# Block products with seven multiplications in place of eight for 18 of 22 up-projection chunks, and product splits moved to the down stage

## The chip, the cores and the metric

The kernel runs on one core of one Trainium2 chip. The metric is the time of one execution on the device in microseconds, as the median of the runs; the profile is of one more execution. The engines are named as in the profile: PE (TensorE, matmuls), DVE (VectorE), ACT (ScalarE), POOL (GpSimd) and SP (SyncE, which here issues the loads).

## The reference

Two layers of a streaming encoder act on 544 rows (512 of a prompt and 32 of a running stream). The first half of a layer (three gated branches and a projection) is untouched by the change. The second half is a gated channel mixer with D_MODEL = 1024 and D_FF = 2816:

```python
f_gate, f_val = jnp.split(x @ w_up, 2, axis=-1)
ffn_ext = jnp.concatenate([ffn_hist.astype(f_gate.dtype), f_gate], axis=1)
f = jax.nn.gelu(causal_dwconv(ffn_ext, ffn_conv_w, ffn_conv_b), approximate=False) * f_val
x = layer_norm(DN_ALPHA * x + f @ w_down, ln2_g, ln2_b)
```

The convolution has width 3 along the rows. All of it is float32.

## The kernel before, in words

**Number format.** Every matmul operand is split into a high part (a copy of type float32r, named wh, xh, fhh) and a low part (the rest: the float32 value minus the high one, named wl, xl, fll). A product is three matmuls into the same PSUM bank: high by high, low x by high weights, high x by low weights (`three`, lines 1683 to 1691). Features lie on the partitions and the 544 rows of x along the free dimension, in two halves of HALF = 272 (dcol(0) and dcol(1)).

**Weight ring.** All weights come as chunks of up to 128 x 2048 float32. SP loads a chunk into `raw[s]` (L339) when the slot is free, ACT copies it to `wh[s]` (`hi`, L505), DVE subtracts into `wl[s]`, which lies on top of `raw[s]` (`lo`, L998), and PE uses it. There are three slots in this stage. POOL makes the low part of one chunk per layer in four pieces of 512 (L482) and is otherwise used for masks, and for four subtractions in the tail (L489).

**Up stage.** An up chunk holds 256 output channels (two tiles of 128, m = 0 and 1) by 1024 inputs (eight tiles). Chunks alternate: a gate chunk, then the value chunk of the same channels; there are 11 pairs per layer. `chunk` on PE makes four units from one: two output tiles by two halves of rows, each 8 x 3 = 24 matmuls into a bank of its own, so 96 per chunk. The first three chunks (gate 0, value 0, gate 1) are taken half by half, because the second half of x is normalised while PE works on the first; the fourth and the 18 that follow are whole.

**Behind a pair.** ACT copies the four gate banks into `gex` (`gate_rows`, L866 to L869), applies the first tap into `cbuf` (`conv_open`, L877), DVE adds the two other taps (`conv_close`, L1551 and L1557), ACT applies the gelu (L881), DVE multiplies with the value banks into `tmp` (`f_products`, L1574 to L1579), ACT copies the high part into `fhh` (`f_rows`, L886) and DVE the low part into `fll` (`f_lows`, L1585). All of it stands in a fixed order written out per engine; ACT and DVE work strictly in that order.

**Down stage.** `down` is called four times per layer (two halves of rows by two halves of the output channels). Each time it takes six chunks (KGROUPS = 3, 4, 3, 4, 4, 4 tiles of inputs) into four banks, 264 matmuls. The first call waits for the products of all pairs but the last before it begins, and for the last pair before its sixth chunk. Then the second layer norm follows beside the calls.

## Time and profile before

| | |
|---|---|
| median of 3 runs | 1798.47 us (1798.11 to 1800.48) |
| span of the profiled execution, first to last instruction | 1796.6 us |
| between that span and the median | 1.9 us |
| PE busy | 1783.3 us, 99% |
| DVE busy | 1141.6 us, 64% |
| ACT busy | 773.2 us, 43% |
| POOL busy | 101.0 us, 6% |
| DMA | 186.00 MB, mean 104 GB/s |

A record of an instruction runs from its start to its end as the profiler saw it. Consecutive records of one engine overlap a little, and matmuls overlap much, so PE's pace is read from counts in a stretch and not from the length of a record. An instruction that is held up by something other than a semaphore has started in the record, so its record is longer; an instruction that waits for a semaphore has not.

### The profile page before, as it was taken

What the parts mean: (1) busy time and instruction counts of PE and PEld (TensorE: products, weight loads), DVE (VectorE), ACT (ScalarE), POOL (GpSimd) and SP (SyncE); (2) the same over time, 40 slices, a digit from 0 to 9 for tenths busy, and PEclk for the clock granted to TensorE, in tenths of its full rate; (3) what the DMA queues carried; (4) which work ended last, traced back from release to release, by engine and by line L of the source; (5) the groups of instructions that cost most, each with busy time, mean ns of one, the idle gap of its engine ahead of it and who ended that gap; (6) DMA issues with size and microseconds to landing.
All of it is one profiled execution on the core that took longest, in us unless ns stands there. A gap on an engine that the chain in (4) does not pass through costs nothing.

```text
span 1796.6 us, 32671 instructions
## 1 busy us (share of the span) xinstructions
PE 1783.3 (99%) x14234; PEld 1749.4 (97%) x14234; DVE 1141.6 (64%) x1745; ACT 773.2 (43%) x1260; POOL 101.0 (6%) x159
## 2 busy tenths in 40 slices
PE   9999999999999999999999999999999999999997
PEld 9998999999999999999999989999999999999997
DVE  5798787755764444446668886786558644445565
ACT  4256533353453344434542564324535534444343
POOL 0025100000100000000000350000001000000000
PEclk9999999999999999999999999999999999999999
DMA  4522122223222222255525221222222222222544
GB/s 172 170 96 72 54 78 83 94 72 116 96 71 82 84 95 95 68 177 181 170 92 169 74 93 38 83 94 78 99 106 71 92 74 94 94 85 94 182 165 137
DMA packets 36511, 186.00 MB, mean 104 GB/s; under 512 B 7376, under 2 KB 11728, under 8 KB 18192
## 3 DMA queue, kind: packets, MB, share of 16 engines
q1 hardware_dynamic: 34672, 176.28, 29.0%
q10 hardware_dynamic: 1696, 7.64, 1.2%
q8 instruction: 112, 1.84, 0.4%
q14 instruction: 31, 0.25, 0.1%
HBM read 176.75 MB, written 7.15 MB: 102 GB/s over the span
## 4 chain that ended last, share of the span: by engine, by line
PE 96%; DVE 3%; issue 1%; DMA 0%; ACT 0%; ACTq 0%; DVEq 0%
PE acc L1685 29%; PE acc L1690 29%; PE acc L1691 29%; PE score L1761 1%; PE small L1812 1%; PE turned L1792 1%; DVE acc L1202 1%; PE score L1690 1%; PE score L1691 1%; PE score L1685 1%; PE turned L1854 1%; PE score L1978 0%; DMA raw<-win 0%; PE small L1827 0%; PE score L1771 0%
## 5 line engine op out<-in xcount | busy, mean ns | idle before, releaser
L1685 PE MATMUL acc<-xh,wh 128*128 128x272 f32 x2944 | 857.0, 291 | 1.5 <-DVE xl L952 1.3
L1690 PE MATMUL acc<-xl,wh 128*128 128x272 f32 x2944 | 847.5, 288 | 0.0
L1691 PE MATMUL acc<-xh,wl 128*128 128x272 f32 x2944 | 847.1, 288 | 0.0
L1685 PEld LDWEIGHTS acc<-xh,wh 128*128 128x128 f32 x2944 | 554.4, 188 | 9.1 <-issue 5.7
L1690 PEld LDWEIGHTS acc<-xl,wh 128*128 128x128 f32 x2944 | 554.2, 188 | 0.1
L1691 PEld LDWEIGHTS acc<-xh,wl 128*128 128x128 f32 x2944 | 553.0, 188 | 0.0
L998 DVE TENSOR_TENSOR wl<-raw,wh 128x2048 fp32r<-128x2048 f32 (+2 forms) x154 | 318.4, 2068 | 215.6 <-ACT wh L505 215.0
L505 ACT ACTIVATE wh<-raw 128x2048 fp32r<-128x2048 f32 (+2 forms) x174 | 305.2, 1754 | 180.5 <-DMA raw<-wdn 132.7
L1685 PE MATMUL acc<-fhh,wh 128*128 128x272 f32 x704 | 204.1, 290 | 0.0
L1691 PE MATMUL acc<-fhh,wl 128*128 128x272 f32 x704 | 202.7, 288 | 0.0
L1690 PE MATMUL acc<-fll,wh 128*128 128x272 f32 x704 | 202.3, 287 | 0.0
L1202 DVE SCALAR_TENSOR_TENSOR acc<-glu,par,acc 128x574 f32<-128x574 f32 x240 | 181.1, 813 | 0.1
L1551 DVE SCALAR_TENSOR_TENSOR cbuf<-gex,par,cbuf 128x546 f32<-128x546 f32 x44 | 34.5, 784 | 197.9 <-ACT cbuf L877 197.9
L1685 PEld LDWEIGHTS acc<-fhh,wh 128*128 128x128 f32 x704 | 132.6, 188 | 0.2
L1690 PEld LDWEIGHTS acc<-fll,wh 128*128 128x128 f32 x704 | 132.5, 188 | 0.2
L1691 PEld LDWEIGHTS acc<-fhh,wl 128*128 128x128 f32 x704 | 132.3, 188 | 0.0
L783 ACT ACTIVATE tmp<-acc,par 128x272 f32<-128x272 f32 x96 | 46.6, 488 | 196.1 <-PE acc L1691 195.7
L1685 PE MATMUL acc<-mh,wh 128*128 128x272 f32 x256 | 74.9, 292 | 0.0
L1691 PE MATMUL acc<-mh,wl 128*128 128x272 f32 x256 | 73.7, 288 | 0.0
L1690 PE MATMUL acc<-ml,wh 128*128 128x272 f32 x256 | 73.7, 288 | 0.0
L886 ACT ACTIVATE fhh<-tmp 128x272 fp32r<-128x272 f32 x88 | 35.2, 431 | 82.0 <-DVE tmp L1579 42.3
L1147 DVE TENSOR_TENSOR_SCAN keep<-keep,zero 128x128 f32<-128x128 f32 (+4 forms) x68 | 58.6, 861 | 15.3 <-POOL beta L471 12.5
(268 smaller groups left out, 2279.2 us busy)
## 6 DMA issues: line engine op xcount, KB each, us to landing
raw<-win SPq DMA_DIRECT2D x50, 1024.0 KB, 4.9
raw<-wup SPq DMA_DIRECT2D x44, 1024.0 KB, 4.9
raw<-wdn SPq DMA_DIRECT2D x32, 1024.0 KB, 4.9
raw<-wbr SPq DMA_DIRECT2D x24, 512.0 KB, 3.6
raw<-wdn SPq DMA_DIRECT2D x16, 768.0 KB, 4.2
raw<-wout SPq DMA_DIRECT2D x8, 1024.0 KB, 4.9
v_out<-vfm ACTq DMA_DIRECT2D x2, 1088.0 KB, 8.7
k_out<-k ACTq DMA_DIRECT2D x2, 1088.0 KB, 4.9
```

Of the source, the lines that this page charges most:

```text
L505: A(wh[s][:, 0:n], raw[s][:, 0:n], ACT.Copy).then_inc(hi_full[s], c.up(hi_full[s]))
L783: A(tmp[:, b, :], ps[b][:, 0:HALF], ACT.Sigmoid, bias=col(par, PAR["b_gate"] + 8 * BRANCHES[n] + 2 * i + b % 2)).then_inc(acc_free[b], c.u ...
L886: A(row(fhh[b // 2], 2 * i + b % 2, 0, HALF), tmp[:, b, :], ACT.Copy).then_inc(f_hi, c.up(f_hi))
L998: v.tensor_tensor(wl[s][:, 0:n], raw[s][:, 0:n], wh[s][:, 0:n].bitcast(F32), ALU.subtract).then_inc(lo_full[s], c.up(lo_full[s]))
L1147: v.tensor_tensor_scan(keep[b][:, T - w:T][:, ::-1], keep[b][:, T - w:T][:, ::-1], zero[:, 0:1].broadcast_to([P, w]), 1.0, ALU.mult, ALU.a ...
L1202: v.scalar_tensor_tensor(out=acc[:, m, :], in0=glu_at(m, j), scalar=w, in1=acc[:, m, :], op0=ALU.mult, op1=ALU.add).then_inc(vec, c.up(vec))
L1551: v.scalar_tensor_tensor(out=cbuf[:, m, :], in0=gex[:, m, 1:GEX - 1], scalar=col(par, PAR["fw"] + FT + t), in1=cbuf[:, m, :], op0=ALU.mult ...
L1685: first = mm(out, a, xs[0], start=start, stop=False)
L1690: mm(out, a, xs[1], start=False, stop=False)
L1691: return mm(out, b, xs[0], start=False, stop=stop)
L1761: last = mm(bs[b][:, 0:w], yc[x][rows, ht, i * P:w], ks[y][rows, ht, 0:w], start=x + y == 0, stop=y == 1)
L1792: last = pe.transpose(bt[:, kb * P:(kb + 1) * P], beta[n % 2][part][:, kb * P:(kb + 1) * P], ident[:, :])
```

## The change

**The products.** 18 chunks per layer (gate 2 to 10 and value 2 to 10) are computed as a 2 x 2 block product. Write the chunk as blocks a11, a12 (output tile 0, first and second four input tiles), a21, a22 (output tile 1), and x as b11, b12 (first four tiles, two halves of rows) and b21, b22. In place of eight block products of four tiles each there are seven (`products`), after sums

```text
s1 = a21 + a22   a3 = a11 - a21   s2 = s1 - a11   s4 = a12 - s2
t1 = b12 - b11   t3 = b22 - b12   t2 = b22 - t1   t4 = b21 - t2
product 1 a11*b11   2 a12*b21   3 s2*t2   4 a3*t3   5 s1*t1   6 s4*b22   7 a22*t4
```

Products 1 and 2 are accumulated in different banks and added by DVE for c11; product 3 is accumulated onto 1, 5 onto 3 and 6 onto 5, with copies m1, u1 and u3 of the bank by ACT in between; 4 has a bank of its own onto which 7 is accumulated (c22 = product 4's bank + u3 is taken by DVE between them, c21 = the bank after 7 + u1). c12 is the bank after product 6. `ORDER` puts products 1 and 2 of the next chunk between 5, 6 and 7 of this one.

**The sums.** The x sums (t1 to t4, each 4 x 272 wide) are made by POOL once per layer when all of x is there, and split by ACT and DVE. The weight sums (s1, a3, s2, s4, each 4 x 128 = 512 wide) are made by POOL per chunk; a3 replaces a21 in `raw[s]`, s1, s2, s4 go to `sraw` and are split by ACT (`shi`) and DVE (`slo`), two at once and then one. The high part of a chunk is two copies of 1024 (second blocks, then first blocks after a3).

**The order.** On ACT per chunk: u3 of the chunk before, high part of the second blocks of the next, m1, c12 of the chunk before, high part of the first blocks, the sums' high parts, u1. On DVE: c22 of the chunk before, c11, first low part of the next, c21 of the chunk before, the other lows. Conv, gelu and gating stand between them.

**The down stage.** The gated products are kept as float32 (`f32`) and split in groups of four tiles (FGROUPS, last one two): for the first half of rows at the end of the up stage, for the second half during the first calls of `down`. `down` waits for the groups it is about to use.

```diff
+QUADS = 18
+ORDER = [(0, 1), (0, 2)]
+for _q in range(QUADS):
+    ORDER += [(_q, 3), (_q, 4), (_q, 5)]
+    ORDER += [(_q + 1, 1)] if _q + 1 < QUADS else []
+    ORDER += [(_q, 6)]
+    ORDER += [(_q + 1, 2)] if _q + 1 < QUADS else []
+    ORDER += [(_q, 7)]
...
+                pool.wait_ge(x_ready[0], 16 + 16 * r)
+                pool.wait_ge(x_ready[1], 16 + 16 * r)
+                x_at = [[xT[:, 4 * k_:4 * k_ + 4, dcol(h)] for h in range(2)] for k_ in range(2)]
+                for n, (j, a, b) in enumerate(((T1, x_at[0][1], x_at[0][0]), (T3, x_at[1][1], x_at[0][1]),
+                                               (T2, x_at[1][1], traw[T1][:, :, :]), (T4N, x_at[1][0], traw[T2][:, :, :]))):
...
+                    g.tensor_tensor(traw[j][:, :, :], a, b, ALU.subtract).then_inc(t_made, 1)
...
+                    pool.wait_ge(raw_full[s], 16 * (SLOT[:j + 1].count(s) - (1 if s < 2 else 0)))
+                    if q > 1:
+                        pool.wait_ge(prod_full, full_at(r, q - 2, 5))
+                    g.tensor_tensor(s1, a21, a22, ALU.add).then_inc(s_made, 1)
+                    pool.wait_ge(s_made, made + 1)
+                    g.tensor_tensor(a21, a11, a21, ALU.subtract).then_inc(s_made, 1)
+                    g.tensor_tensor(s2, s1, a11, ALU.subtract).then_inc(s_made, 1)
+                    pool.wait_ge(s_made, made + 3)
+                    if q > 1:
+                        pool.wait_ge(prod_full, full_at(r, q - 2, 6))
+                    g.tensor_tensor(s4, a12, s2, ALU.subtract).then_inc(s_made, 1)
```

On PE, `products` waits at the head of a product:

```diff
+                    if p == 2:
+                        pe.wait_ge(lo_full[blocks[q]], c.take(lo_full[blocks[q]]))
...
+                    if p == 3:
+                        pe.wait_ge(snapped, act_at(r, "m1", q))
+                        pe.wait_ge(s_ready, sums + 1)
...
+                    if p == 5:
+                        pe.wait_ge(snapped, act_at(r, "u1", q))
+                    if p == 6:
+                        pe.wait_ge(snapped, act_at(r, "u3", q))
+                        pe.wait_ge(s_ready, sums + 2)
+                    if p == 7:
+                        pe.wait_ge(combined, dve_at(r, "c22", q))
```

On DVE, at the first pairs and at the end of the stage:

```diff
                 history(0)
                 conv_close(0)
                 f_products(0, FIRST_VALUE)
                 lo()
-                f_lows(0)
-                for i in range(10):
...
+                turned_x_lo()
+                history(1)
+                first_low(0)
+                skip(range(4))
+                conv_close(1, range(2), False)
+                other_lows(0)
+                f_products(1)
...
+                for g_ in range(1, 3):
+                    f_lows(0, g_)
+                lo()
+                for g_ in range(3, 6):
+                    f_lows(0, g_)
```

On PE, in `down`:

```diff
-                        if h == 0 and j == len(KGROUPS) - 1:
-                            pe.wait_ge(f_ready, c.seen(f_ready))
+                        groups = [g_ for g_, (a, b) in enumerate(FGROUPS) if a < at + kn]
+                        pe.wait_ge(f_ready, 12 * r + 6 * h + groups[-1] + 1)
```

The order of the instructions shows three places. On POOL, behind the low part of the chunk that it had before (wl), there were the masks of the next layer:

```order
L482 TENSOR_TENSOR wl_60<-raw_57,wh_54 128x512 [waits hi_full2]
L482 TENSOR_TENSOR wl_60<-raw_57,wh_54 128x512 x3
L462 AFFINE_SELECT wsgu<-wsgu 128x512 [waits late_full]
L471 AFFINE_SELECT keep_111<-keep_111 128x128 [waits sig_full0]
L471 AFFINE_SELECT beta_113<-beta_113 128x128
```

and now the x sums (traw) and the weight sums (sraw, and raw in place for a3) stand between them:

```order
L546 TENSOR_TENSOR wl_60<-raw_57,wh_54 128x512 x3
L556 TENSOR_TENSOR traw_101<-xT 128x1088 [waits x_ready1,x_ready0]
L556 TENSOR_TENSOR traw_100<-xT 128x1088
L556 TENSOR_TENSOR traw_99<-xT,traw_101 128x1088 [waits t_made]
L556 TENSOR_TENSOR traw_102<-xT,traw_99 128x1088 [waits t_made]
L569 TENSOR_TENSOR sraw_105<-raw_55 128x512 [waits raw_full0]
L571 TENSOR_TENSOR raw_55<-raw_55 128x4x128 [waits s_made]
L572 TENSOR_TENSOR sraw_105<-sraw_105,raw_55 128x512
L576 TENSOR_TENSOR sraw_105<-raw_55,sraw_105 128x512 [waits s_made]
```

The four of a chunk come 18 times per layer, from the third chunk on with waits for prod_full too. On DVE a pair in the middle of the stage was

```order
L1557 SCALAR_TENSOR_TENSOR cbuf<-gex,par,cbuf 128x546 [waits vec]
L998 TENSOR_TENSOR wl_58<-raw_55,wh_52 128x2048 [waits hi_full0]
L1574 TENSOR_TENSOR tmp<-acc,cbuf 128x272 [waits fgelu_full,acc_full0]
L1574 TENSOR_TENSOR tmp<-acc,cbuf 128x272 [waits fgelu_full,acc_full1]
L1577 TENSOR_TENSOR tmp<-acc,cbuf 128x240 [waits acc_full2]
L1579 TENSOR_TENSOR tmp<-acc,cbuf 128x32
L1577 TENSOR_TENSOR tmp<-acc,cbuf 128x240 [waits acc_full3]
L1579 TENSOR_TENSOR tmp<-acc,cbuf 128x32
L1585 TENSOR_TENSOR fll_87<-tmp,fhh_85 128x272 [waits f_hi] x2
L1585 TENSOR_TENSOR fll_88<-tmp,fhh_86 128x272 [waits f_hi] x2
L998 TENSOR_TENSOR wl_59<-raw_56,wh_53 128x2048 [waits hi_full1]
```

and of one chunk now, from the gating products on (f is the float32 product, small and turned are banks, m and u the copies by ACT):

```order
L1845 TENSOR_TENSOR f_89<-f_89,cbuf 128x544 [waits fgelu_full,snapped,combined]
L1846 TENSOR_TENSOR f_90<-f_90,cbuf 128x2x240
L1847 TENSOR_TENSOR f_90<-f_90,cbuf 128x2x32
L1813 TENSOR_TENSOR wl_58<-raw_55,wh_52 128x1024 [waits s_made]
L1818 TENSOR_TENSOR slo_108<-sraw_106,shi_104 128x1024 [waits s_hi]
L1818 TENSOR_TENSOR slo_108<-sraw_106,shi_104 128x512 [waits s_hi]
L1826 TENSOR_TENSOR gex<-small,u_0_111 128x240 [waits snapped,prod_full]
L1827 TENSOR_TENSOR gex<-small,u_0_111 128x32
L1837 TENSOR_TENSOR f_89<-acc,m_1_112 128x272 [waits snapped,prod_full]
L1806 TENSOR_TENSOR wl_59<-raw_56,wh_53 128x1024 [waits s_made,hi_full1]
L1837 TENSOR_TENSOR gex<-small,u_0_110 128x272 [waits snapped,prod_full]
```

One low part of 2048 has become three of 1024 and one of 512 with waits between them, and the narrow products and splits have gone. At the end of the stage, DVE goes from the last chunk to the down chunks (wl of 2048 is the second down chunk) in this order:

```order
L1837 TENSOR_TENSOR f_89<-turned,u_1_113 128x272 [waits snapped,prod_full]
L1845 TENSOR_TENSOR f_89<-f_89,cbuf 128x544 [waits fgelu_full,snapped,combined]
L1846 TENSOR_TENSOR f_90<-f_90,cbuf 128x2x240
L1847 TENSOR_TENSOR f_90<-f_90,cbuf 128x2x32
L1788 TENSOR_TENSOR fll_87<-f_89,fhh_85 128x1088 [waits f_hi] x2
L1199 TENSOR_TENSOR wl_59<-raw_56,wh_53 128x2048 [waits hi_full1]
L1788 TENSOR_TENSOR fll_87<-f_89,fhh_85 128x1088 [waits f_hi] x2
```

Before, both low parts of the first two down chunks stood ahead of the last pair's products. PE has 13203 rows in its order, where it had 13635.

## Rows read from the trace of the kernel before

**Rows 1.** Page of the profile: busy time per engine, and the chain that ended last.

```profile
PE 1783.3 (99%) x14234; PEld 1749.4 (97%) x14234; DVE 1141.6 (64%) x1745; ACT 773.2 (43%) x1260; POOL 101.0 (6%) x159
...
PE 96%; DVE 3%; issue 1%; DMA 0%; ACT 0%; ACTq 0%; DVEq 0%
```

**Rows 2.** Stretches of the up stage: busy us of PE, PEld, DVE, ACT, POOL; clock, DMA.

```profile
545.10:761.60 216.50, 216.50 (x1729) 216.50 (x1729) 100.90 (x199) 88.43 (x144) 0.00 (x0) 1.00 0.25 87
1433.60:1650.00 216.40, 216.40 (x1729) 216.40 (x1728) 100.74 (x200) 88.67 (x145) 0.00 (x0) 1.00 0.25 87
```

**Rows 3.** DVE groups by form (busy us, mean ns), and four rows in order of time.

```profile
L998 DVE TENSOR_TENSOR wl<-raw,wh 128x1024 fp32r<-128x1024 f32 x24 | 29.3, 1221 | 14.7 <-ACT wh L505 14.7
L1551 DVE SCALAR_TENSOR_TENSOR cbuf<-gex,par,cbuf 128x546 f32<-128x546 f32 x44 | 34.5, 784 | 197.9 <-ACT cbuf L877 197.9
L1125 DVE TENSOR_TENSOR sq<-xT,st 128x544 f32<-128x544 f32 x32 | 21.9, 725 | 0.4
L1048 DVE TENSOR_TENSOR xT<-xT,small 128x1088 f32<-128x1088 f32 x8 | 10.2, 1280 | 0.0
...
617.75 1.49 DVE L1585 TENSOR_TENSOR fll<-tmp,fhh 128x272 fp32r<-128x272 f32 x4
```

**Rows 4.** ACT groups by form (busy us, mean ns).

```profile
L505 ACT ACTIVATE wh<-raw 128x2048 fp32r<-128x2048 f32 x134 | 256.1, 1911 | 121.3 <-DMA raw<-wdn 94.2 <-DMA raw<-win 20.3 <-DMA raw<-wout 4.6
L505 ACT ACTIVATE wh<-raw 128x1024 fp32r<-128x1024 f32 x24 | 25.3, 1054 | 20.7 <-DMA raw<-wbr 20.7
L639 ACT ACTIVATE wh<-raw 128x512 fp32r<-128x512 f32 x4 | 2.5, 627 | 2.4 <-DMA raw<-win 2.4
L866 ACT ACTIVATE gex<-acc 128x272 f32<-128x272 f32 x40 | 15.6, 396 | 51.3 <-PE acc L1691 51.3
```

**Rows 5.** POOL's pieces at 484 us and DVE beside them (start, us), and one DVE line.

```profile
484.19 1.66 POOL L482 TENSOR_TENSOR wl<-raw,wh 128x512 fp32r<-128x512 f32 x1 [296.61 <-ACT wh L505]
485.81 1.49 POOL L482 TENSOR_TENSOR wl<-raw,wh 128x512 fp32r<-128x512 f32 x1
488.50 1.28 POOL L482 TENSOR_TENSOR wl<-raw,wh 128x512 fp32r<-128x512 f32 x1
...
483.98 0.73 DVE L1037 TENSOR_TENSOR cbuf<-xT 128x544 f32<-128x544 f32 x1
484.74 1.41 DVE L1039 TENSOR_TENSOR st<-cbuf 128x272 f32<-128x272 f32 x1
...
L1039 DVE TENSOR_TENSOR st<-cbuf x8: 441/443/1418, 458.6 to 1751.8; 128x272 f32<-128x272 f32 x8
```

**Rows 6.** Loads of the up weights: count, size, median us from issue to landing.

```profile
raw<-wup SPq DMA_DIRECT2D x44, 1024.0 KB, 4.9
```

**Rows 7.** The tail: POOL's subtractions and DVE beside them.

```profile
1785.82 1.29 POOL L489 TENSOR_TENSOR xT<-xT,cbuf 128x272 f32<-128x272 f32 x1 [407.79 <-ACT cbuf L938]
1788.99 0.75 POOL L489 TENSOR_TENSOR xT<-xT,cbuf 128x272 f32<-128x272 f32 x1
...
1786.42 0.43 DVE L1111 TENSOR_TENSOR st<-turned,st 128x272 f32<-128x272 f32 x1
1786.77 0.93 DVE L1116 TENSOR_TENSOR xT<-xT,cbuf 128x544 f32<-128x544 f32 x1
```

**Rows 8.** Start of the up stage: DVE, and ACT's read of a gate bank.

```profile
514.58 0.44 DVE L1131 TENSOR_TENSOR xl<-xT,xh 128x272 fp32r<-128x272 f32 x1 [0.57 <-ACT xh L543]
...
522.42 0.79 DVE L1551 SCALAR_TENSOR_TENSOR cbuf<-gex,par,cbuf 128x546 f32<-128x546 f32 x1 [7.24 <-ACT cbuf L877]
...
528.38 2.29 DVE L998 TENSOR_TENSOR wl<-raw,wh 128x2048 fp32r<-128x2048 f32 x1 [0.47 <-ACT wh L505]
...
533.07 0.37 ACT L868 ACTIVATE gex<-score 128x240 f32<-128x240 f32 x1 [2.54 <-PE score L1691]
```

**Rows 9.** End of the up stage: DVE's low part of the second down chunk.

```profile
758.25 2.29 DVE L998 TENSOR_TENSOR wl<-raw,wh 128x2048 fp32r<-128x2048 f32 x1 [0.86 <-ACT wh L505]
```

More of the change, by code:

```diff
@@ L1542, in _, with conv_close @@
                 low_tiles(1, range(KT))
[L1545 to L1548 removed]
+                def conv_close(i, tiles=range(2), counted=True):
+                    if counted:
+                        skip(range(4))
+                    for m in tiles:
                         t = 2 * i + m
@@ new lines, in left @@
+                def left(q, m):
+                    i = 2 + q // 2
+                    bank, add = (PA[q % 2], snap[q % 2]["m1"]) if m == 0 else (PC[q % 2], snap[q % 2]["u1"])
+                    dve.wait_ge(prod_full, full_at(l, q, 7 if m else 2))
+                    dve.wait_ge(snapped, act_at(l, "u1" if m else "m1", q))
+                    out = gex[:, m, 2:2 + HALF] if q % 2 == 0 else f32[0][:, 2 * i + m, :]
+                    v.tensor_tensor(out, bank[:, 0:HALF], add[:, :], ALU.add).then_inc(combined, 1)
@@ L2040, in _, with products @@
                 chunk()
-                for r in range(9):
-                    chunk()
-                    chunk()
+                blocks = {}
+                def products(n):
+                    q, p = ORDER[n]
+                    bank = {1: PB, 6: PB, 7: PC, 2: PA, 3: PB, 4: PC, 5: PB}[p][q % 2]
+                    sums = 2 * (r * QUADS + q)
+                    if p == 1:
+                        blocks[q] = arrived()
+                        if q > 1:
+                            pe.wait_ge(snapped, act_at(r, "c12", q - 2))
+                    if p == 2:
+                        pe.wait_ge(lo_full[blocks[q]], c.take(lo_full[blocks[q]]))
+                        if q > 1:
+                            pe.wait_ge(combined, dve_at(r, "c11", q - 2))
+                        else:
+                            pe.wait_ge(acc_free[q], c.seen(acc_free[q]))
+                    if p == 3:
+                        pe.wait_ge(snapped, act_at(r, "m1", q))
+                        pe.wait_ge(s_ready, sums + 1)
+                        if q == 0:
+                            pe.wait_ge(t_ready, 4 * (r + 1))
+                    if p == 4 and q > 1:
+                        pe.wait_ge(combined, dve_at(r, "c21", q - 2))
+                    if p == 5:
[5 more added lines that the diff above has]
+                        pe.wait_ge(combined, dve_at(r, "c22", q))
+                    s, half = blocks[q], q % 2
+                    for t in range(4):
+                        if p in (1, 2, 4, 7):
+                            at = {1: t * 256, 2: (4 + t) * 256, 4: t * 256 + P, 7: (4 + t) * 256 + P}[p]
+                            w = [x[s][:, at:at + P] for x in (wh, wl)]
+                        else:
+                            w = [x[half][:, {5: 0, 3: 1, 6: 2}[p], t * P:(t + 1) * P] for x in (shi, slo)]
+                        if p in (1, 2, 6):
+                            tile, h = {1: (t, 0), 2: (4 + t, 0), 6: (4 + t, 1)}[p]
+                            mv_ = [x[:, tile, dcol(h)] for x in xs]
+                        else:
+                            mv_ = [x[{3: T2, 4: T3, 5: T1, 7: T4N}[p]][:, t, :] for x in (th, tl)]
+                        last = three_of(bank[:, 0:HALF], w, mv_, p in (1, 2, 4) and t == 0, t == 3, p not in (1, 2, 4))
+                    last.then_inc(prod_full, 1)
+                    if p == 7:
+                        read.append(s)
@@ L2046, in down @@
+                for n in range(len(ORDER)):
+                    products(n)
+                pe.wait_ge(combined, dve_at(r, "c11", QUADS - 1))
                 def down(h, middle=None):
```

314 lines of the change are left out of this document (265 added, 49 removed).

## The prediction, made before the change was timed

> **What bounds the kernel now.** I read the busy times of the page first. TensorE (PE) is busy in 99% of the span and the chain that ended last runs 96% through it [rows 1]; every other engine has slack on average. Then the stretches of the up stage [rows 2]: in the first layer PE fills all of 545.1 to 761.6 us, and the second layer repeats it from 1433.6 to 1650.0. These 216.5 us are 18 chunks of 96 matmuls, so a matmul costs 216.5 / 1728 = **0.1253 us**, and a chunk 12.03 us. The granted clock is 1.00 there, the upper level of 2.4 GHz, and PE did not pause. POOL does nothing in that stretch, DVE is busy 100.9 and ACT 88.4 of 216.5 us. So a matmul taken out is worth its 0.1253 us as long as the other engines keep up with the new, shorter chunk.
>
> **What is taken out.** A chunk is a 2 by 2 block product (two halves of the input rows by two output tiles, with two column halves). Eight block products of 12 matmuls become seven: 84 matmuls, 10.52 us. Per layer 18 x 12 x 0.1253 = **27.06 us**, for two layers 54.1. The order of the instructions agrees: PE has 432 rows fewer.
>
> **What is added, engine by engine, for one chunk of 10.52 us.** "Takes" is a record less the 0.08 us by which neighbours overlap, as where four 272-wide DVE rows of 0.43 us take 1.49 [rows 3].
> - ACT: 88.4 / 18 = 4.9 us a chunk before. The high half of 2048 (1.91 us) becomes two of 1.05, and the sums of 1024 and 512 add 1.05 and 0.63 [rows 4]; the bank reads (0.40) are about as many as before. That is 6.8 us of 10.52, off the path.
> - DVE: two lows of 1024 (1.22), lows of the sums of 1024 and 512 (1.22, 0.69), three additions that read PSUM (0.44, as the 272-wide row of rows 5), and per pair four conv steps (0.79), gating products of 544, 480 and 64 (0.73 for 544, estimated 0.66 and 0.2) and small copies [rows 3]. Taken together 7.6 us.
> - POOL: four additions or subtractions of 512. The nearest row is its own low half of 512, 1.28 us alone, one every 1.24 [rows 5]. That is 5.0 us.
> - DMA: one load of 1 MB per chunk as before, 4.9 us to landing [rows 6]. The slot is freed at product 7 and the sums are first wanted three products (4.5 us) later, so POOL starts some 0.4 us late; it is inside the POOL chain below.
>
> No engine is full by itself. **But DVE and POOL get in each other's way.** At 484.19 us POOL begins its first piece while DVE runs a 544-wide subtraction until 484.71. The piece takes 1.66 instead of 1.28 us and ends at 485.85. DVE's next addition (272 wide, both inputs in SBUF) starts at 484.74 and takes 1.41 instead of 0.44 us: it ends at 486.15, 0.30 us after the piece. POOL's second piece then ends at 487.30, 1.15 after that [rows 5]. The tail repeats it (DVE 0.93 instead of 0.73 us beside POOL's 272-wide subtractions, 1.29 instead of 0.75 [rows 3, 7]). So an instruction of POOL and a DVE instruction with two SBUF inputs exclude each other; a hold is 1.15 us for POOL's 512, and for DVE its record less about 0.13. DVE instructions that read a PSUM bank are not held (0.43 at 1786.42, beside POOL [rows 7]).
>
> Per chunk the holds are: POOL 4 x 1.15 = 4.6; DVE lows 3 x 1.09 + 0.56 = 3.8, conv 2 x 0.66 = 1.3, gating 0.6 (half a pair), 5.7 together. **10.3 of 10.52 us**: the pair is full to 98%. The Trainium skill ("SBUF — State Buffer", section "SBUF: two separate sides") says that of such a pair whichever starts first has the shared ports for the whole instruction. Read as whole records, that rule would make 11.8 us of the 10.3; the trace agrees that one blocks the other, and differs in the length, since DVE ends 0.30 us behind the piece where its record alone is 0.44 [rows 5].
>
> What does the 98% cost PE? By the bounds: nothing, if the waits fall in DVE's own pauses; and if DVE stood still through all of POOL's holds, its chunk would be 7.6 + 4.6 = 12.2 us, 1.7 over PE's. About 1.5 us of DVE's work (the PSUM additions and the copies) can run beside POOL, which leaves 10.7, 0.2 over. I take **0.35 us** a chunk: those 0.2 and 0.15 for moments in which both wait for a product. PE would show it before product 7 (it needs the bottom-right addition of DVE) and before product 5 (it needs ACT's copy u1, which is queued behind the high halves of POOL's sums). The last two chunks of a layer have no sums beside them, so 16 x 0.35 = 5.6 us per layer.
>
> **The start of the stage.** POOL now makes four combinations of x, 1088 wide, as soon as the last low tile of x is there (515.0 [rows 8]). From its 512 and 272 wide rows (1.28 and 0.75 alone, 2.2 ns an element) one takes an estimated 2.4 to 2.5 us, so they last until 524.6, and the eight sums of two chunks follow without pause. DVE's four conv steps of the first pair start at 522.4 [rows 8] and each now waits for one POOL instruction, 2.2 + 3 x 1.15 = 5.7 us. Behind them stand ACT's gelus, ACT's high half and DVE's low half of the second value chunk, which was ready at 530.67 for a unit that PE began when the one before ended, at 533.07 [rows 8]: 2.4 us of slack. So PE waits 3.3 us (bounds: 0 if POOL is slower to start than the conv, 5.7 if it also collides with the low half). Behind that, ACT and DVE still have the splits of the combinations to do, but 12 us of units cover them.
>
> **The end of the stage.** Before, the low half of the second down chunk ran at 758.25 and was done 1.1 us before the stage ended [rows 9]. Now it stands behind the last product. From the last product's end DVE does: latency 0.2, bottom-left addition 0.4, gating products 1.4, two splits of four tiles (1088 wide, 1.2 each, from the 1.28 of the same width [rows 3]), the low half 2.2. That is 6.6 us; PE has 36 matmuls of the first down chunk, 4.5 us. **2.1 us** of wait (0 to 3.5). The other product splits are cheaper than before (six wide ones for 22 narrow) and covered by the down stage's passes of 264 matmuls, 33 us each.
>
> **The sum.** Per layer 27.06 - 5.6 - 3.3 - 2.1 = 16.06 us, twice 32.1. The profiled span is 1796.6 us, and 1.9 us lie between it and the median 1798.47, which I carry along: 1764.5 span, **1766.4 us**.
>
> **Rivals.**
> 1. *The exclusion hides.* For it: DVE was idle for more than half of the up stage [rows 2], and the additions have two chunks of lead. Against: 98%. Then only the 2.1 us at the end stay: 1798.5 - 2 x (27.06 - 2.1) = 1748.6 us.
> 2. *An instruction holds for its whole record*, its fixed part included: POOL 4 x 1.28 and DVE 6.7 (three of 1.22, 0.69, two of 0.79, gating 0.8) make a chunk of 11.8 us, 1.3 over PE's. Per layer 27.06 - 16 x 1.3 - 5.4 = 0.9, so 1796.7 us, no difference. The row of 484.74 is against it. It is what the page of the Trainium skill named above would make of it.
> 3. *The chain through POOL sets the pace*, and the kernel is slower. Place: product 5 of chunk q - 2 ends, POOL does four operations, ACT the last high half and u1, and only then product 5 of chunk q - 1 may start. Besides POOL this chain has 0.2 + 0.6 + 0.4 + 0.4 for the late load + 1.6 for the product, 3.2 us; it keeps PE's pace if POOL needs under 7.3 us. Alone it needs 5.0; if each operation also waits for one DVE low (1.09) it needs 4 x (1.15 + 1.09) = 9.0, a chunk of 12.2 us. Per layer 27.06 - 16 x 1.7 - 5.4 = -5.5, so 1809.5 us. It turns to a loss at a chunk of 11.9, POOL at 8.7 us. For it: POOL here reads blocks with gaps, which no row shows, and it collides at every step. Against: of DVE's nine holds in a chunk at least half fall outside these 7 us.
>
> That the change does not do what it says is ruled out by the order's 432 rows. Met waits at the head of each product are counted at nothing: the stage before has four of them a chunk, and PE is busy in 216.50 of 216.50 us [rows 2].
>
> **Chances.** Forecast (0.1 to 0.9 us lost per chunk) 0.55, rival 1 0.25, rival 2 0.07, rival 3 0.13. A measurement of this kernel can tell about 0.2%, 3.6 us. Faster by more: 0.55 + 0.25 + 0.03 of rival 2 (it stands at the bound) = 0.83; within: 0.04 of rival 2 and 0.02 from the mild end of rival 3; slower 0.11. Range: down to 1746, 2.6 us under rival 1 for an end that hides too; up to 0.95 us lost per chunk, 2 x 16 x 0.6 = 19 us over the forecast, 1786. Rivals 2 and 3 stay outside.
>
> **What would show it.** Right: PE has 84 matmuls in 10.7 to 11.0 us in the middle of the stage; POOL's 512-wide rows read 1.3 to 2.3 us, not 1.28, and DVE's 1024-wide lows up to 2.4 instead of 1.22; PE waits before a product on DVE (small or turned) or ACT (u1), together 5 to 6 us per layer, and once 2 to 4 us near the second value chunk and about 2 us on the low half of the second down chunk. Wrong: POOL at 1.28 throughout (rival 1); a chunk over 11.5 us with ACT's u1 as the releaser (rival 3); POOL over 1.6 us where no DVE instruction runs beside it, which my prices do not have.

## The result and the profile after

The changed kernel takes **1813.36 us** (median of four runs, 1811.58 to 1816.19) where the kernel before took 1798.36 beside it: a ratio of 1.0084, 95% interval 1.007 to 1.0098. It is slower; 1766.4 was predicted, with 0.11 on slower. The profiled span is 1810.6 us, 14.0 over the span before, where 54.1 us of matmuls had been taken out. So 68 us went elsewhere, 34 per layer; the prediction had allowed 11.

The page after (busy time, and the chain that ended last), against [rows 1]:

```profile
PE 1754.7 (97%) x13802; PEld 1709.7 (94%) x13802; DVE 1348.9 (75%) x1869; ACT 850.5 (47%) x1366; POOL 345.0 (19%) x311
...
PE 74%; DVE 12%; issue 4%; DMA 4%; ACT 3%; POOL 3%; ACTq 0%; DVEq 0%; POOLq 0%
```

PE did lose work, but it is busy for 97% and no longer 99% of the span, and the chain leaves it for a quarter of the way, mostly to DVE. PE's waits after (engine line waited for: us in total, times, longest us); before, the whole list came to 2.7 us:

```profile
PE score L1978 <- ACT u L1016: 21.4, 18, 2.5
PE acc L1978 <- ACT gex L962: 6.4, 2, 3.2
PE acc L1978 <- DVE wl L1199: 6.2, 5, 2.1
PE acc L1978 <- DVE f L1777: 6.2, 2, 3.7
```

A wait costs PE somewhat more than the list says, since the first matmul starts late too: 1.14 us in the list is a start 1.43 us behind the start before it, 1.30 more than the usual 0.125.

**In the middle of the stage** PE stops once per pair of chunks, before product 6 of the odd chunk:

```profile
622.14 0.29 PE L1984 MATMUL score<-xh,wl 128*128 128x272 f32 x1
623.57 0.39 PE L1978 MATMUL score<-xh,shi 128*128 128x272 f32 x1 [1.14 <-ACT u L1016]
```

The next such stop begins at 645.16. A pair thus takes 23.02 us, a chunk 11.51: the change wanted 10.52 and the kernel before took 12.03. **0.99 us a chunk** is lost where 0.35 was priced. Of the 2.0 us of a pair the stop and the slow start behind it are 1.4; the rest are stops of 0.1 to 0.3 us before product 7 and before product 5. What stood ahead of the wait is seen on three engines (start, us, in order of time). DVE:

```profile
615.83 2.35 DVE L1806 TENSOR_TENSOR wl<-raw,wh 128x1024 fp32r<-128x1024 f32 x1 [0.48 <-POOL sraw L572]
...
618.45 1.21 DVE L1813 TENSOR_TENSOR wl<-raw,wh 128x1024 fp32r<-128x1024 f32 x1
619.58 1.81 DVE L1818 TENSOR_TENSOR slo<-sraw,shi 128x1024 fp32r<-128x1024 f32 x2
621.32 0.23 DVE L1767 COPY gex<-fhist 128x2 f32<-128x2 f32 x2
622.54 0.86 DVE L1753 SCALAR_TENSOR_TENSOR cbuf<-gex,par,cbuf 128x546 f32<-128x546 f32 x1 [1.00 <-ACT cbuf L1034]
```

ACT:

```profile
621.66 1.58 ACT L1034 ACTIVATE cbuf<-gex,par 128x546 f32<-128x546 f32 x2 [3.32 <-DVE gex L1767]
623.15 0.37 ACT L1016 ACTIVATE u<-score 128x272 f32<-128x272 f32 x1
```

POOL:

```profile
615.80 1.28 POOL L576 TENSOR_TENSOR sraw<-raw,sraw 128x512 f32<-128x512 f32 x1
621.54 1.28 POOL L569 TENSOR_TENSOR sraw<-raw 128x512 f32<-128x512 f32 x1 [4.45 <-DMA raw<-wup]
```

POOL's 615.80 holds DVE's low part, 2.35 us instead of 1.21. From there DVE's queue runs on without pause, so the tiny history copies (L1767), which stand last in it, come at 621.32. ACT has been idle for 3.32 us with its next instruction, the first tap of the conv (L1034), waiting for them. Behind the two taps on ACT stands u3, and on u3 waits product 6.

The groups show how far the exclusion reaches. DVE after, by form (busy us, mean ns); the last two are copies of two columns, the same work, 0.16 us each in the kernel before. They stand one behind the other, so that the first bears the whole hold:

```profile
L1806 DVE TENSOR_TENSOR wl<-raw,wh 128x1024 fp32r<-128x1024 f32 x36 | 60.4, 1677 | 7.3 <-POOL sraw L572 7.3
...
L1756 DVE COPY fst<-gex 128x2 f32<-128x2 f32 x44 | 33.5, 762 | 0.0
L1757 DVE COPY fst<-gex 128x2 f32<-128x2 f32 x44 | 6.9, 156 | 0.0
```

POOL's sums take means of 1.41 to 1.69 us, 6.2 for the four of a chunk; two of the four groups:

```profile
L569 POOL TENSOR_TENSOR sraw<-raw 128x512 f32<-128x512 f32 x36 | 60.6, 1685 | 204.3 <-DMA raw<-wup 158.1 <-PE score L1984 46.2
L572 POOL TENSOR_TENSOR sraw<-sraw,raw 128x512 f32<-128x512 f32 x36 | 50.8, 1412 | 0.0
```

**At the start and the end** PE waits three times per layer. In the first layer (start, us):

```profile
536.87 0.57 PE L1978 MATMUL acc<-xh,wh 128*128 128x272 f32 x1 [3.21 <-ACT gex L962]
555.82 0.36 PE L1978 MATMUL acc<-xh,wh 128*128 128x272 f32 x1 [2.51 <-DVE f L1777]
770.69 0.39 PE L1978 MATMUL acc<-fhh,wh 128*128 128x272 f32 x1 [2.12 <-DVE wl L1199]
```

Measured from start to start these are 3.50, 2.80 and 2.41 us (3.46, 3.94 and 2.42 in the second layer). ACT and DVE around the first two:

```profile
531.40 4.09 ACT L982 ACTIVATE th<-traw 128x1088 fp32r<-128x1088 f32 x4
535.40 1.04 ACT L993 ACTIVATE wh<-raw 128x1024 fp32r<-128x1024 f32 x1
536.35 0.66 ACT L962 ACTIVATE gex<-acc 128x272 f32<-128x272 f32 x2
```

```profile
533.74 9.21 DVE L1795 TENSOR_TENSOR tl<-traw,th 128x1088 fp32r<-128x1088 f32 x4
546.97 1.25 DVE L1756 COPY fst<-gex 128x2 f32<-128x2 f32 x1
```

Behind some of these waits PE runs at its lower clock level. One window of the profile after (busy us of PE, PEld, DVE, ACT, POOL; granted clock, DMA):

```profile
496.00:545.00 49.00, 45.61 (x336) 44.69 (x335) 39.25 (x53) 27.25 (x46) 21.91 (x10) 0.93 0.19 65
```

### The profile page after: what moved, and what is told of

Read it like the earlier page. It is cut to its first block, busy times and chain, and to the rows that moved or that the text cites. A ratio compares the mean times of both kernels' runs of the same rounds, so it can differ in the third digit from the quotient of the medians.

```text
span 1810.6 us, 32645 instructions
## 1 busy us (share of the span) xinstructions
PE 1754.7 (97%) x13802; PEld 1709.7 (94%) x13802; DVE 1348.9 (75%) x1869; ACT 850.5 (47%) x1366; POOL 345.0 (19%) x311
## 4 chain that ended last, share of the span: by engine, by line
PE 74%; DVE 12%; issue 4%; DMA 4%; ACT 3%; POOL 3%; ACTq 0%; DVEq 0%; POOLq 0%
PE acc L1978 21%; PE acc L1984 20%; PE acc L1983 20%; DMA raw<-wup 3%; PE score L1978 2%; DVE slo L1818 2%; PE score L1984 2%; PE score L1983 2%; POOL sraw L569 1%; PE score L2054 1%; DVE wl L1199 1%; PE small L2105 1%; PE turned L2085 1%; DVE wl L1813 1%; DVE cbuf L1753 1%
## 5 line engine op out<-in xcount | busy, mean ns | idle before, releaser
L1978 PE MATMUL acc<-xh,wh 128*128 128x272 f32 x1936 | 570.6, 295 | 14.0 <-ACT gex L962 6.4
L1984 PE MATMUL acc<-xh,wl 128*128 128x272 f32 x1936 | 560.9, 290 | 0.0
L1983 PE MATMUL acc<-xl,wh 128*128 128x272 f32 x1936 | 559.9, 289 | 0.0
L1978 PEld LDWEIGHTS acc<-xh,wh 128*128 128x128 f32 x1936 | 367.5, 190 | 22.4 <-issue 18.3
L1199 DVE TENSOR_TENSOR wl<-raw,wh 128x2048 fp32r<-128x2048 f32 (+2 forms) x118 | 236.0, 2000 | 179.4 <-ACT wh L601 178.8
L1983 PEld LDWEIGHTS acc<-xl,wh 128*128 128x128 f32 x1936 | 367.7, 190 | 0.1
L1984 PEld LDWEIGHTS acc<-xh,wl 128*128 128x128 f32 x1936 | 366.7, 189 | 0.0
L1978 PE MATMUL score<-th,shi 128*128 128x272 f32 x288 | 85.4, 297 | 2.2 <-ACT u L1016 2.2
L1984 PE MATMUL score<-th,slo 128*128 128x272 f32 x288 | 83.5, 290 | 0.0
L1983 PE MATMUL score<-tl,shi 128*128 128x272 f32 x288 | 83.0, 288 | 0.0
```

The lines of the kernel that those rows point to most:

```text
L1199: v.tensor_tensor(wl[s][:, 0:n], raw[s][:, 0:n], wh[s][:, 0:n].bitcast(F32), ALU.subtract).then_inc(lo_full[s], c.up(lo_full[s]))
L1978: first = mm(out, a, xs[0], start=start, stop=False, skip_group_check=onto)
L1983: mm(out, a, xs[1], start=False, stop=False, skip_group_check=onto)
L1984: return mm(out, b, xs[0], start=False, stop=stop, skip_group_check=onto)
```

## The experiments

Two things were in question. One is the exclusion between POOL and DVE: seen rightly, but under-priced. The other is the new order of the work (history copies last on DVE, taps ahead of u3 on ACT), which might cost the time by itself, with or without POOL. Each expectation says what its own A and B are. The four runs with memsets are single executions; the four runs of the change lie up to 4.6 us apart, so differences of 1 us between single runs say nothing.

**The exclusion taken away, the order kept.** POOL takes as long as its sums would take alone, in steps with the same waits, but as memsets, which read nothing. From the third chunk on the weight sums are not computed.

```diff
+                    if q >= 2:
+                        for n in range(4):
...
+                            pool.wait_ge(s_made, made + n)
+                            g.memset(scratch[:, 0:680], 0.0).then_inc(padded, c.up(padded))
+                            pool.wait_ge(padded, c.seen(padded))
+                            g.memset((s1, scratch[:, 0:512], s2, s4)[n], 0.0).then_inc(s_made, 1)
+                        return
```

> From the third chunk of a layer on POOL's four sums are replaced by pairs of memsets of the same length (about 1.3 us a pair, with the same semaphores), which read nothing; the weight sums are not computed. Theory B: with nothing of POOL to exclude, DVE is on time, the chunk falls from 11.5 to 10.5 us and the time by 32 x 1.0 = 31 us to about 1782. Theory A: DVE runs some 1 us per chunk earlier, so the history copies and u3 come earlier too, but they still stand behind the lows that wait for POOL's last sum; at most half of the loss goes, 1798 us or more.

1778.71 us, 34.7 less than the change. A pair of memsets takes what a sum took alone, start to start 1.31 us (5.2 us for the four, where the held sums needed 6.2):

```profile
626.23 0.67 POOL L576 MEMSET scratch<- 128x680 f32 x1 [5.69 <-DMA raw<-wup]
626.96 0.53 POOL L578 MEMSET sraw<- 128x512 f32 x1
627.54 0.67 POOL L576 MEMSET scratch<- 128x680 f32 x1
```

DVE's low part after a3 is back at the price of [rows 3], and PE's waits on ACT's copies are 3.0 us where they were 21.4 (line numbers are 11 higher here: the two copies are L1756 and L1757 of the change):

```profile
L1817 DVE TENSOR_TENSOR wl<-raw,wh 128x1024 fp32r<-128x1024 f32 x36 | 43.8, 1217 | 3.8 <-POOL sraw L578 3.8
L1767 DVE COPY fst<-gex 128x2 f32<-128x2 f32 x44 | 19.8, 451 | 0.0
L1768 DVE COPY fst<-gex 128x2 f32<-128x2 f32 x44 | 18.5, 419 | 0.0
...
PE score L1989 <- ACT u L1027: 3.0, 4, 0.8
```

The exclusion from the third chunk on is worth 17.3 us per layer (half of 34.7), against 5.6 priced. The Trainium skill ("SBUF — State Buffer", section "Who interferes with whom") says that a DVE instruction with two SBUF inputs contends with a GpSimd instruction that reads SBUF and not with one that only writes, and that a copy can run in a mode in which it contends with GpSimd whatever that does. The run agrees on both: 1677 ns fell to 1217, but the two copies, 762 and 156 ns in the change, are at 451 and 419. Together they still take 870 ns, where they took 918, and 0.32 us before. So the memsets free all of DVE but its copies.

**The same, and the history copies early.**

```diff
                     if q < QUADS:
                         left(q, 0)
+                    if q % 2 == 0 and q < QUADS:
+                        dve.wait_ge(conv3_full, c.seen(conv3_full))
+                        history(2 + q // 2)
                     first_low(q + 1)
...
                     if q % 2:
-                        history(2 + q // 2)
```

> Both edits: history copies early, and POOL's sums replaced by memsets of the same length (weight sums not computed). Both theories: every wait inside the stage goes, a chunk of 10.5 us, and only the waits at the start (about 3.4 and 3.3 us), at the end (2.4) and the half-rate stretches behind them stay: about 1782 us. If it is clearly above, there is a third cause in the chain of POOL, ACT and PE itself.

1779.71 us with the memsets, no gain. Once POOL's reads hold nobody, the order costs nothing, so it is not a cause by itself. Whether it decides how much of the holds reaches PE is the question of the next run.

**The history copies early, POOL as in the change.**

> Only DVE's two history copies (2 columns each) into gex move: from behind the low parts of the next chunk to right after the addition for c11 of the even chunk. Theory A (the steady loss is an ordering: the copies are last in DVE's queue, ACT's taps wait for them, u3 stands behind the taps, product 6 waits for u3): the 1.43 us gap before product 6 of every odd chunk goes, 8 pairs x 2 layers x about 1.4 us = 22 us, so about 1791 us. Theory B (POOL and DVE exclude each other and DVE is simply late): the taps start earlier but DVE stays late, another wait (product 5 or 7) takes its place, and at most 8 us are won, 1805 us or more.

1801.59 us, ratio to the kernel before 1.0013 (1.0004 to 1.0022): 12 us won, between the two expectations. The wait before product 6 is gone, and two others have come:

```profile
PE score L1980 <- ACT u L1016: 14.7, 15, 1.1
PE small L1980 <- DVE gex L1827: 2.9, 12, 0.9
```

The first is now before product 5, on u1. At one such place (ACT, then POOL, then DVE):

```profile
626.10 0.66 ACT L1039 ACTIVATE cbuf<-cbuf 128x546 f32<-128x546 f32 x1 [1.92 <-DVE cbuf L1759]
626.67 1.04 ACT L1005 ACTIVATE shi<-sraw 128x1024 fp32r<-128x1024 f32 x1
628.13 0.38 ACT L1016 ACTIVATE u<-score 128x272 f32<-128x272 f32 x1
```

```profile
623.49 1.66 POOL L576 TENSOR_TENSOR sraw<-raw,sraw 128x512 f32<-128x512 f32 x1
```

```profile
620.44 1.81 DVE L1759 SCALAR_TENSOR_TENSOR cbuf<-gex,par,cbuf 128x546 f32<-128x546 f32 x1
622.52 1.47 DVE L1753 SCALAR_TENSOR_TENSOR cbuf<-gex,par,cbuf 128x546 f32<-128x546 f32 x1
623.92 1.26 DVE L1756 COPY fst<-gex 128x2 f32<-128x2 f32 x1
```

POOL's last sum was there at 625.15, and ACT could not take it, since the gelu ahead of it in its queue waited for DVE's conv, in which POOL had held two steps and two copies. Of the 16 odd chunks from chunk 3 on (counted from 0), ACT takes the last sum 2.1 to 2.5 us after POOL has made it in 13; in the even ones it takes it at once and then waits for PE. So it is not POOL's chain that is long; DVE is full. The same 23 us of the stage in this run, in the memset run and in the change (busy us of PE, PEld, DVE, ACT, POOL; clock, DMA):

```profile
604.20:627.20 23.00, 21.69 (x171) 21.25 (x169) 22.41 (x29) 13.05 (x22) 12.52 (x8) 1.00 0.28 95
```

```profile
604.20:627.20 23.00, 23.00 (x185) 23.00 (x184) 17.29 (x31) 14.19 (x24) 10.46 (x18) 1.00 0.28 94
```

```profile
604.20:627.20 23.00, 21.86 (x170) 21.26 (x169) 20.26 (x29) 12.74 (x22) 12.16 (x9) 1.00 0.27 93
```

DVE's records fill 22.41 of 23.00 us in the first, 5.1 more than in the memset run. In the change it is 20.26, with pauses in which ACT's taps run. In the memset run PE is never idle.

The 12 us did not come from the pairs in the middle of the stage. The first matmul of product 6 of chunks 5 and 15 in this run (in the change they start at 623.57 and 739.05):

```profile
619.75 0.29 PE L1980 MATMUL score<-xh,shi 128*128 128x272 f32 x1
...
734.38 0.29 PE L1980 MATMUL score<-xh,shi 128*128 128x272 f32 x1
```

That is 11.46 us a chunk, and 11.55 in the change; six chunks of the second layer give 11.42 and 11.48. With the copies early more of DVE's instructions run into POOL's: over one pair the held records exceed their price alone by 7.2 us together, where it was 5.0 in the change. So what were pauses is now filled with holds. The bulk of the 12 us lies in the first pairs of each layer (3.4 and 2.6 us between product 6 of chunk 0 and that of chunk 5), at the end of the second layer's stage (2.9, where a wait of 2.82 us with a stretch at half rate is gone).

**The start.** All 18 chunks with memsets, the x sums real (the weight sums are not computed):

```diff
-                    if q >= 2:
+                    if q >= 0:
```

> POOL's weight sums of all 18 chunks are memset pairs of equal length (they read nothing, the weight sums are not computed); the x sums stay real. With the earlier run in which the first two chunks kept real sums (1778.7) and the one in which the x sums were memsets too (1761.4) it splits the loss at the start. Theory A (the second wait comes from DVE's low parts of the x sums, 9.2 us for four, each held by POOL's eight sums of the first two chunks): they take 5.1 us now, the second wait of 3.9 goes, the first (ACT's splits wait for POOL's late x sums, which collide with the conv) stays at 2 to 3.5: 1767 to 1771. Rival B (it comes from the late x sums alone): both waits stay, 1776 to 1779.

1768.66 us, 10.1 less than with two chunks left real. DVE's four low parts of the x sums and PE's first wait:

```profile
533.43 4.89 DVE L1806 TENSOR_TENSOR tl<-traw,th 128x1088 fp32r<-128x1088 f32 x4
...
536.56 0.36 PE L1989 MATMUL acc<-xh,wh 128*128 128x272 f32 x1 [3.22 <-ACT gex L973]
```

They take 4.89 instead of 9.21 us. The second wait is gone, the first stands. So the second is made by the weight sums of the first two chunks, which the prediction had all but over by then: it let them follow the x sums "without pause", but POOL waited for the load of that chunk until 532.67 and so met the low parts.

Then the x sums as memsets of equal length too (neither kind of sum is computed):

```diff
-                    g.tensor_tensor(traw[j][:, :, :], a, b, ALU.subtract).then_inc(t_made, 1)
+                    for w in (760, 760):
+                        g.memset(scratch[:, 0:w], 0.0).then_inc(padded, c.up(padded))
+                        pool.wait_ge(padded, c.seen(padded))
+                    g.memset(traw[j][:, :, :], 0.0).then_inc(t_made, 1)
```

> As the memset run, with all of POOL's work of this stage replaced by memsets of equal length: the x sums and the sums of the first two chunks too (no block sums are computed). If the two waits at the start of the stage (3.5 us on ACT's read of a gate bank, 3.9 us on DVE's products of the second value chunk) come from the exclusion as well, the first falls to about 1 us and the second goes, with the stretches at half rate behind them: 2 x (2.5 + 3.9 + 1 to 2) less than the 1778.7 us of the memset run, 1762 to 1766 us. If they come from the order in ACT's and DVE's queues, it stays at 1775 us or more.

1761.37 us, another 7.3 less; the first wait falls from 3.50 to 1.47 us. The exclusion, but for the copies, is thus worth 52.0 us, 26 per layer. What is left, 17.1 us of span over 1796.6 - 54.1, is there without it, 1.47 us of the first wait too.

ACT's gate reads ahead of the splits of the x sums, in the change itself:

```diff
+                for b in range(2):
+                    gate_rows(b, SECOND_GATE[b])
                 turned_x_hi()
                 second_blocks(0)
-                for b in range(4):
+                for b in range(2, 4):
                     gate_rows(b, SECOND_GATE[b])
```

> ACT reads the first two gate banks of the second pair ahead of the splits of the x sums and of the high half of the next chunk; nothing else is changed. Theory A (the two waits at the start are one delay that is handed on: the DVE low parts of the x sums, 9.2 us for four, stand in both): the first wait falls from 3.5 to about 0.5 us and the second grows by about as much (2.8 and 3.9 to 6 to 7), so the time stays within 3 us of the change, 1810 to 1816. Rival B (the second wait has causes of its own, ACT's order was the whole of the first): the second stays 2.8 to 3.9, 3 us are won per layer and the half-rate stretch behind the first goes too: 1803 to 1807.

1813.07 us, no difference. The first wait fell to 0.46 us, the second grew to 8.45 in both layers, from 2.80 and 3.94 (in the list, two waits on DVE's f of 16.3 us together). The waits are one delay that is handed on; with no stop before it, PE only reaches the second place earlier.

Gates early, DVE's products of the second value chunk ahead of its other low parts, history early and the end of the next paragraph, all at once:

> The history copies early, and three more moves: ACT reads the first two banks of the second gate chunk before it splits the x sums, DVE takes the products of the second value chunk before the low parts of the sums, and the second down chunk's high and low halves go before the last chunk's work. Theory A plus the reading of the trace (the waits of 3.5, 2.8 to 3.9 and 2.4 us at the edges come from these three places, and each is followed by a stretch at half rate that costs 1.4 to 2.5 us more): 1791 less 2 x (3.4 + 2.4 + 1.6 for the half rate) or more, 1775 us; 1768 if the second wait goes as well. Rival for the edges: DVE is behind by the excluded time and only the releaser changes, 1785 or more.

1797.89 us, 0.9994 (0.9984 to 1.0003): 3.7 less than with history early alone, which is about what the end is worth. At the start the wait became one of 7.69 us per layer, on another low part. Moving work about does not help while DVE is held.

**The end.** Both parts of the second down chunk split ahead of the last chunk's additions, the low one on DVE as shown, the high one on ACT likewise:

```diff
+                    if q == QUADS:
+                        lo()
                     first_low(q + 1)
...
                 for g_ in range(1, 3):
                     f_lows(0, g_)
-                lo()
```

> Only the end of the stage is changed: both halves of the second down chunk are split ahead of the last chunk's additions. Theory A (the term of the end stands by itself): the wait on wl of 2.4 us becomes one of 1.25 on the split of the products, as where this was done with other edits; 1.2 us are won per layer, and the half-rate stretch behind the wait (about 1.3 us lost) goes too: 5 us in all, 1807 to 1810. Rival B (the time lost at half rate is not owed to the length of the wait): 2.4 us in all, 1810.5 to 1812.

1809.26 us, 1.0061 (1.0044 to 1.0077), 4.1 less than the change. The wait is 1.28 us in place of 2.41. This is 2.3 us for two layers; the half-rate stretch behind the wait is gone too, but the change had one in the first layer only (last section), 1.4 us. The sum is 3.7. That it comes so near to 4.1 is in part chance: elsewhere this trace has a half-rate stretch that is longer by 1.2 us and lacks the wait of 2.82.

**Less for POOL to do.** History early, and s2 and s4 made by DVE. POOL keeps s1 and a3:

```diff
-                    g.tensor_tensor(s2, s1, a11, ALU.subtract).then_inc(s_made, 1)
...
-                    g.tensor_tensor(s4, a12, s2, ALU.subtract).then_inc(s_made, 1)
...
+                def own_sums(q):
...
+                        v.tensor_tensor(s2, s1, a11, ALU.subtract).then_inc(s_dve, 1)
+                        dve.wait_ge(s_dve, 2 * (l * QUADS + q) + 1)
+                        v.tensor_tensor(s4, a12, s2, ALU.subtract).then_inc(s_dve, 1)
```

> History copies early, and two of the four weight sums of a chunk (s2 and s4) are made by DVE in place of POOL. Exclusion theory, with the holds read before the change: POOL 2 x 1.15 and DVE 5.7 + 2 x 0.55 are 9.1 us in place of 10.3 for a chunk of 10.52, while DVE has 8.8 us of work of its own in place of 7.6. Most of the steady waits go, 1801.6 less some 20: 1778 to 1786 us. If what counts is DVE's amount of work, the time rises above 1801.6; if it is the length of the chain from product 5 through POOL, it falls too, but the memset run (same length of chain, no waits) speaks against that.

1777.07 us, 0.988 (0.9867 to 0.9894): 24.5 less than history early alone, and faster than before. DVE, the engine that was full, got two more instructions a chunk (0.69 us each), and the kernel became faster, because each takes one of POOL's holds away: over the whole kernel DVE's records come to 1362.5 us, and to 1374.4 with history early alone, though 49.8 us of work were added to them. POOL's chain is shorter here too; that this was not the limit rests on the last sums that waited for ACT above, not on this run.

History early and the x sums made by DVE, which is idle there; ACT's splits of them move ahead of its last gate reads of the first pair (not shown):

```diff
                 history(0)
+                turned_x()
+                turned_x_lo()
                 conv_close(0)
                 f_products(0, FIRST_VALUE)
                 lo()
-                turned_x_lo()
```

> History copies early, and the four x sums are made and split on DVE and ACT in the 7 us in which DVE was idle before the first conv step, in place of POOL beside the conv steps. Only the start of the stage changes: the waits of 3.5 and 3.9 us and the half-rate stretches behind them go or shrink to under 2 us, 1801.6 less 2 x 7 to 10 us: 1782 to 1788 us. If the backlog at the start is made by the weight sums of the first two chunks, at most the first wait goes: 1792 us or more.

1792.77 us, 0.9965 (0.9952 to 0.9979), 8.8 less than history early alone. The first wait is 0.83 us, the second stays (3.77), which is what was expected if the weight sums of the first two chunks cause it.

**All of it: the version to keep.** History early, s2, s4 and the x sums on DVE, the end early:

> The candidate: history copies early, s2 and s4 and the x sums on DVE, and the second down chunk's halves ahead of the last chunk's work. If the three readings add up: 1798.5 - 54.1 + 2 x (about 2 us of steady waits, 0 to 2 at the start, 1.1 at the end) = 1750 to 1758 us. If the effects do not add, above 1765 us.

**1765.88 us, 0.9824 (0.9811 to 0.9837)**, with the same results computed. It beats the kernel before by 1.8% and the change by 2.6%. Hoped for was 1750 to 1758, and above 1765 was to mean that the effects do not add. The parts measured singly say otherwise: 1801.59 - 24.5 - 8.8 - 4.1 = 1764.2. They add up to within 1.7 us, and the expectation had the parts too large: a chunk takes 10.96 us (mean of thirteen in the first layer), 0.44 over PE's, which makes 7 us per layer of steady waits and not 2. Its page and its largest wait:

```profile
PE 1737.3 (99%) x13802; PEld 1698.5 (96%) x13802; DVE 1367.4 (78%) x1949; ACT 854.9 (48%) x1366; POOL 222.4 (13%) x231
...
PE small L1993 <- DVE gex L1836: 6.1, 7, 1.0
```

## Why the prediction was wrong

Per layer the prediction took 11.0 us off the 27.06; it was 34 to 35. By the differences between the runs they divide so (us; the start is the last two memset steps and what is left of the first wait; the last row is what is left in all):

| | predicted | measured |
|---|---|---|
| middle of the stage | 5.6 | 17.3 |
| start | 3.3 | 10.1 |
| end | 2.1 | 2.3 |
| not in the sum | 0 | 4.9 |

**Right: what is taken out.** 27.06 us per layer. In the memset run PE is busy in 23.00 of 23.00 us. Nothing of the gain was lost to the matmuls themselves.

**Right: the cause, and the prices of the single instructions.** DVE and POOL exclude each other, POOL's 1088-wide pieces took 2.5 to 2.8 us (2.4 to 2.5 estimated; the prediction's own 2.2 ns an element give 2.55), the 512-wide ones 1.28 where free, DVE's lows 1.22 where free and 2.35 where held, as forecast under "what would show it". DVE's own work was right too: with history early a pair takes 22.93 us, less 7.2 of holds and 0.5 of a wait for POOL that is 7.6 us a chunk.

**Wrong, the step that failed: "I take 0.35 us a chunk".** It was 0.99. The step took the pair of engines as a capacity (98% full, so a little waits) and then looked for the waits before products 5 and 7 only. Three things were left out of it:
- The wait that came is before product 6, through history copy, tap and u3. DVE's and ACT's fixed orders turn any lateness of DVE into lateness of ACT: ACT is busy for 12.7 of 23.0 us and still late. This fixes where PE waits, and in the middle of the stage hardly how long: with the two copies moved the chunk fell by 0.06 to 0.09 us only.
- The small copies were counted as free of holds. L1756's take 762 ns, not 156.
- The bound of 12.2 us, in which DVE stands still through all of POOL's holds, had been drawn down to 10.7 by letting 1.5 us of DVE's work (PSUM additions and copies) run beside POOL. With history early DVE stands still through 3.6 of the 4.6 us that POOL's four sums hold, and waits 0.25 for POOL: 7.6 + 3.6 + 0.25 = 11.45, and 11.46 is measured.

Per layer this is 17.3 us by the memset run and not 5.6 (16 times 0.99 is 15.8; the difference also holds a wait of 2.82 us and half-rate stretches). By the prediction's own sum a chunk that loses 0.99 us would still have given 1786.9 us. So this step alone leaves a small gain; what makes it a loss is the start and what was not in the sum.

**The size of the first wait right by luck, the mechanism not: "So PE waits 3.3 us".** The first wait is 3.50 and 3.46 us. But the conv was held back by 2.5 us and not 5.7 (from DVE's first step at 523.04 to ACT's last gelu at 529.03 it is 5.99 us, before it was 3.46), since POOL's weight sums did not follow the x sums: they waited for their load. And PE waited for ACT's gate reads behind the splits of the x sums (4.1 us) and a high part (1.0), not for DVE's low half; 1.47 us of it stay when POOL holds nobody. **Wrong: "12 us of units cover them".** DVE's four low parts took 9.21 us and not 5, and a second wait of 2.80 and 3.94 us followed. The start cost 7.3 + 10.1 us by the memset runs, 8.7 per layer, and 1.4 more are there without the exclusion.

**Right: the end.** 2.1 us predicted, 2.41 and 2.42 measured, on the low half that was named.

**Not in the sum.** Half-rate stretches, six in the two layers, some 9 us (below; five of them lie behind waits of the start and the middle and are counted there by the memset runs); two further waits per layer that remain with every sum a memset, 0.79 us before the last product 6 and 0.75 on a down chunk's low part; and about 3 us in gaps too short to be listed (the 17.1 us left in that run, less 11.0 of its longer waits and 3.0 at half rate). What makes the last was not tried.

**The rivals.** Rival 3 gave 1809.5 us, near the 1813.36, by a mechanism that was not there: POOL needs 6.2 us of the 7.3 allowed it, and where u1 did become the last (history early), POOL's last sum had been ready for 1.5 us when ACT came to the sums. Its sign, a chunk over 11.5 us with u1 as the releaser, came only half: 11.51, with u3. Its chance of 0.13 was the only weight on the right side. Rival 2 gave a chunk of 11.8, nearer to the 11.5 than the forecast's 10.87, though holds are not whole records: the conv of 622.54 ended at 623.40, only 0.58 us behind the POOL record beside which it had started, where it takes 0.79 alone [rows 3]. Rival 1, in which the exclusion hides, is what the last memset run should come near to; it took 1761.37 for 1748.6. So even without the exclusion 12.8 us were missing from the sum.

## What to carry to other kernels

Two engines that exclude each other are one resource, and a forecast that finds it 98% full should start from the bound where one of them does its own work and then stands through the other's (12.2 us here, 11.5 measured), and not from a full overlap of what can overlap. The smallest instruction at the end of a queue that another engine's queue waits for, here a copy of two columns, shows where the wait comes out; moving it wins little where the resource itself is full. And work moved onto the seemingly idle partner may cost more there than on the busy engine: taking two of four sums back from POOL made the kernel 24.5 us faster.

## What was not expected of the hardware

**Half rate after a wait of a few microseconds.** After 536.87 us the matmuls start every 0.227 us with records of 0.43 instead of every 0.125 with 0.29, until 542.67; that is the lower of the clock's two levels, 1.2 GHz in place of 2.4. The granted clock of the window of 49 us reads 0.93, and 5.4 us at half of it would make 0.94:

```profile
539.04 0.43 PE L1978 MATMUL acc<-xh,wh 128*128 128x272 f32 x1
539.27 0.43 PE L1983 MATMUL acc<-xl,wh 128*128 128x272 f32 x1
...
542.84 0.29 PE L1984 MATMUL acc<-xh,wl 128*128 128x272 f32 x1
542.97 0.29 PE L1978 MATMUL acc<-xh,wh 128*128 128x272 f32 x1
```

In the change six waits are followed by this (3.50, 2.80, 2.41, 3.46, 3.94 and 2.83 us), each for 11 to 24 matmuls, 91 in all at 0.10 us: 9 us. The length of the wait does not settle it: a wait of 2.42 us in the second layer has none behind it, nor has one of 2.55 in the run with the gates early, where one of 2.04 has. In the version kept, whose waits in the stage are 1.26 us at most, there is none. The Trainium skill ("TensorE: Matmul & The Clock Gate", section "Part 1: The HAM clock gate (the "warmup" mystery)") has the two levels, 1.2 and 2.4 GHz. The two paces of the rows agree with them roughly: 0.227 and 0.125 us are 1.8 to 1, not 2 to 1.

**A copy of two columns waits for a whole instruction of POOL:** 1.25 us at 546.97, and 2.51 beside a 1088-wide one, where it takes 0.16 alone. Memsets on POOL hold it too, for up to 0.75 us, and then often both copies of a pair (451 and 419 ns on average).
